# Two-layer encoder on one core: the first output tile beside the last heads, and the norms by halves of the positions

## The reference, cut to what matters

```
mods   = silu(c) @ ada_w + ada_b                 # shifts, scales, gates: rows of channels
layer 0:  h = rmsnorm(x, g) * (1 + scale) + shift
          x = x + gate1 * (forgetting_attention(h) @ w_o)   # 16 heads, causal, bias F_i - F_j
          h = rmsnorm(x, g) * (1 + scale) + shift
          x = x + gate2 * ((silu(conv(h Wg)) * conv(h Wv)) @ w_down)   # 2816 hidden channels
shared:   h = modulated rmsnorm(x);  k, v = h @ kv_w        # 4 heads of 64 channels
layer 1:  q = modulated rmsnorm(x) @ w_q
          x = x + gate1 * (sliding_window_attention(q, k, v, alibi, sinks) @ w_o)
          x = x + gate2 * conv_ffn(modulated rmsnorm(x))
out    =  rmsnorm(x, g)
```

## Time and profile before

| what | us |
|---|---|
| device time, median of three runs | 2446.96 |
| the three runs | 2446.95, 2446.96, 2448.36 |
| device time of the profiled execution | 2450.65 |
| span of the profiled execution in the trace | 2448.8 |
| PE busy | 2309.4 |
| DVE busy | 1535.8 |
| POOL busy | 1173.5 |
| ACT busy | 1147.6 |

### The profile page before, as it was taken

One profiled execution on the slowest core, in us unless ns is written; L12 is line 12 of the kernel. 1 busy time (PEld: TensorE's weight loads), 2 busy tenths in 40 slices (PEclk: granted clock), 3 DMA queues, 4 the chain that ended last, 5 costly groups with the idle time before them and its releaser, 6 DMA issues.

```text
span 2448.8 us, 30449 instructions
## 1 busy us (share of the span) xinstructions
PE 2309.4 (94%) x10984; PEld 1922.2 (78%) x10984; DVE 1535.8 (63%) x2470; ACT 1147.6 (47%) x1934; POOL 1173.5 (48%) x1580
## 2 busy tenths in 40 slices
PE   5999999998989999999999899989899999999996
PEld 3778788886767888888888688878678888888884
DVE  6575656657677677777665686882564444545546
ACT  4475665748145333333333476771443333333334
POOL 5411313120546766666666352214366666666650
PEclk8999999999999999999999999989999999999998
DMA  7111211112831333333331313133111111111111
GB/s 266 53 48 35 69 35 55 42 56 78 309 112 42 117 121 121 121 125 123 124 119 59 127 34 77 53 110 122 35 43 52 52 52 57 56 52 52 52 52 69
DMA packets 66007, 206.91 MB, mean 84 GB/s; under 512 B 7345, under 2 KB 7985, under 8 KB 65730
## 3 DMA queue, kind: packets, MB, share of 16 engines
q1 hardware_dynamic: 29760, 109.06, 14.0%
q10 hardware_dynamic: 36098, 95.91, 12.0%
HBM read 186.66 MB, written 16.32 MB: 83 GB/s over the span
## 4 chain that ended last, share of the span: by engine, by line
PE 80%; DVE 9%; ACT 6%; DMA 3%; issue 2%; SPq 0%; POOL 0%; ACTq 0%; DVEq 0%
PE bank L917 50%; PE bank L632 19%; PE bank L792 1%; PE bank L766 1%; DVE H L1658 1%; PE bank L827 1%; PE bank L802 1%; PE bank L1088 1%; PE bank L828 1%; PE bank L829 1%; ACT PF L1226 1%; DMA ada_raw<-in_ada_t 1%; PE bank L648 1%; DVE tn L1653 1%; DVE ada_raw L1669 1%
## 5 line engine op out<-in xcount | busy, mean ns | idle before, releaser
L917 PE MATMUL bank<-H,w_spl 128*128 128x512 f32 x3744 | 872.3, 392 | 19.3 <-DVE H L1658 14.6
L917 PEld LDWEIGHTS bank<-H,w_spl 128*128 128x128 f32 x3744 | 708.0, 189 | 171.7 <-issue 16.2
L561 POOL TENSOR_TENSOR w_spl<-w_raw,w_spl 128x256 fp32r<-128x256 f32 x688 | 536.7, 808 | 426.7 <-ACT w_spl L1380 425.2
L632 PE MATMUL bank<-H,w_spl 128*128 128x512 f32 x2016 | 509.9, 401 | 19.1 <-DVE H L1658 11.6
L917 PE MATMUL bank<-TB,w_spl 128*128 128x512 f32 x2112 | 492.6, 389 | 0.0
L917 PEld LDWEIGHTS bank<-TB,w_spl 128*128 128x128 f32 x2112 | 396.1, 188 | 83.3 <-issue 0.8
L632 PEld LDWEIGHTS bank<-H,w_spl 128*128 128x128 f32 x2016 | 378.4, 193 | 98.1 <-issue 12.6
L1380 ACT ACTIVATE w_spl<-w_raw 128x512 fp32r<-128x512 f32 x328 | 196.8, 624 | 356.3 <-PE bank L917 300.5
L499 POOL TENSOR_TENSOR pace<-one_s 128x1 f32<-128x1 f32 x50 | 13.1, 262 | 682.9 <-PE bank L792 350.5
L1934 DVE SCALAR_TENSOR_TENSOR X<-bank,mods,X 128x1024 f32<-128x1024 f32 x176 | 225.2, 1280 | 45.5 <-PE bank L917 44.7
L1927 DVE TENSOR_TENSOR bank<-bank,sU 128x512 f32<-128x512 f32 x80 | 55.9, 699 | 302.6 <-PE bank L917 302.6
(11 more groups left out here) (172 smaller groups left out, 3180.1 us busy)
## 6 DMA issues: line engine op xcount, KB each, us to landing
w_raw<-in_w_stream SPq DMA_DIRECT2D x184, 512.0 KB, 3.7
ada_raw_f<-in_ada_t ACTq DMA_DIRECT2D x128, 256.0 KB, 2.9
ada_raw_o<-in_ada_t ACTq DMA_DIRECT2D x8, 2048.0 KB, 7.7
ada_raw<-in_ada_t SPq DMA_DIRECT2D x8, 1024.0 KB, 18.9
negF<-scratch_f ACTq DMA_DIRECT2D x16, 512.0 KB, 3.7
X<-in_x_t SPq DMA_DIRECT2D x4, 1024.0 KB, 10.9
X<-in_x_t ACTq DMA_DIRECT2D x4, 1024.0 KB, 8.3
scratch_x<-X ACTq DMA_DIRECT2D x1, 4096.0 KB, 12.7
```

Source lines behind the costliest of these rows:

```text
L561: last = pool.tensor_tensor(block_at(layer, b, 1, q, q + 256), src[:, q:q + 256], block_at(layer, b, 0, q, q + 256).bitcast(F32), ALU.subt ...
L632: last = pe.matmul(dst, stat(k, a), mov(k, b), start=(k == 0 and a + b == 0), stop=(k == KT - 1 and a == 1))
L917: last = pe.matmul(dst, block_at(layer, b, x, k * P, k * P + P), mov(y), start=(start and x + y == 0), stop=(stop and x == 1), skip_group_ ...
```

## The change

1. **Heads.** All heads take one plan of maxima (MAX_T), the negated maxima always at t = 8, and four of the 32 fill steps move from the second head of a group to the first (FILL_1).
2. **The last group.** From T = 20 POOL makes the high parts PH (POOL_HIGH), in parts of 256 columns, in ACT's place. O is loaded (HEADS_LOADS) and split (HEADS_SPLITS) earlier, straight into H's place. PE puts seven of the eight k-steps of the output projection's tile 0 (six matmuls each) beside the tasks (OUT_A_BESIDE); out_two then makes tile 1 and ends both. POOL's weight tiles from the fourth of w_o on come after its high parts.
3. **Output projections.** Tiles 6 and 7 go by halves of the positions (out_last), and the sum of the first half's squares, its root, its norm and its modulation begin before the second halves are done; the FFN's first pair also goes by halves, with the second half's sum inside it. Tiles 4 to 7 make three rows of mods instead of four; the four others go into FFN pairs 2 and 3 as half rows, and the other half rows move from pairs 3 to 18 to pairs 4 to 19 (ada_steps).
4. **FFN entry.** The taps of hidden tile 0 move ahead of the last two of the four T sums, on ACT and DVE; hidden tile 0's split moves behind the copy that S4 waits for.
5. **FFN end and K/V.** The last down product goes by halves in a ring of four banks (last_down), residuals by halves, POOL adds the squares (add_squares, two operations of 256 columns for each), and the norm and the K/V product go by halves. This norm writes X × rstd into X itself, so that the norm for Q has no multiplication. SP stores X in halves before that, and loads bias_s, both of which were on ACT's queue.
6. **The end.** DVE multiplies X by gain and rstd in one operation into Y, in 16 halves, and SP issues 16 DMAs of 256 KB.

```diff
-MAX_T = [[2, 1, 1, 1, 1, 1, 1, 2, 2, 0, 0, 0], [0, 0, 2, 1, 2, 1, 2, 1, 2, 1, 0, 0]]
-MAX_T.append(MAX_T[0])
+MAX_T = [2, 1, 1, 1, 1, 1, 1, 2, 2, 0, 0, 0]
...
-FILL_1 = [2] * 16
+FILL_1 = [3] * 4 + [2] * 10
...
+POOL_HIGH = 20
+HEADS_LOADS = {13: (0, 1, 2), 14: (3, 4, 5), 34: (6,)}
+HEADS_SPLITS = {16: 0, 18: 1, 20: 2, 22: 3, 24: 4, 26: 5, 41: 6}
+OUT_A_BESIDE = {25: (0,), 28: (1,), 31: (2,), 34: (3,), 37: (4,), 40: (5,), 44: (6,)}
...
+def ada_steps(p):
+    if p in (2, 3):
+        return 4 * (p - 2), 4, p - 2, p == 2
+    if 4 <= p < 20:
+        return 8 + 8 * (p - 4), 8, int(p < 12), p < 12
+    return 136, 0, 0, False
...
+            def store_x(h):
+                for j in range(4):
+                    sp.wait_ge(dn_ev, 80 + 8 * h + 2 * j + 2)
+                    sp.dma_start(dX.rearrange("k p s -> p k s")[:, 2 * j:2 * j + 2, half_of(h)],
+                                 X[:, 2 * j:2 * j + 2, half_of(h)]).then_inc(x_out[h], 16)
             for pos in range(3, W_TILES):
+                if pos in (W_KV + 2, W_KV + 3):
+                    store_x(pos - W_KV - 2)
+                if pos == W_KV + 3:
+                    sp.dma_start(bias_s[:], alibi).then_inc(bias_in, 16)
...
+            for h in range(2):
+                for kt in range(KT):
+                    sp.wait_ge(y_done, 8 * h + kt + 1)
+                    sp.dma_start(out_t[kt, :, half_of(h)], Y[:, kt, half_of(h)]).then_inc(y_out, 16)
+            sp.wait_ge(y_out, 16 * 16)
...
+            for T in range(POOL_HIGH, 4 * NT):
+                n_task = 4 * NT * (NG - 1) + T
+                n = task_span(T % NT)[1]
+                pool.wait_ge(p_exp, n_task + 1)
+                for q in range(0, n, 256):
+                    last = pool.tensor_scalar(PH[n_task % NP][:, q:min(n, q + 256)], PF[n_task % NP][:, q:min(n, q + 256)],
+                                              1.0, 1.0, ALU.mult, ALU.mult)
+                last.then_inc(p_hi, 1)
+            for pos in range(W_OUT_A + 3, W_FFN[0]):
+                tile(pos)
...
+            def add_squares(n, m, h):
+                pool.wait_ge(sq_done, SQ_0[n] + 8 * h + m + 1)
+                first = ss[:, half_of(h)]
+                if m == 1:
+                    first = sq_at(n, 0, h)
+                else:
+                    pool.wait_ge(ss_done, SS_0[n] + 6 * h + m - 1)
+                for q in (0, 256):
+                    last = pool.tensor_tensor(ss[:, h * HALF + q:h * HALF + q + 256], first[:, q:q + 256],
+                                              sq_at(n, m, h)[:, q:q + 256], ALU.add)
+                last.then_inc(ss_done, 1)
...
+            def square_sum(n, h):
+                at_end = n == 4 and h == 1
+                pe.wait_ge(ss_done, SS_0[n] + (6 * h + 6 - at_end if n in (2, 4) else 6 + h))
+                pe.matmul(bank(h), ones[:], ss[:, half_of(h)], start=True, stop=False)
...
+                pe.wait_ge(sq_done, SQ_0[n] + (8 * h + 8 if n in (2, 4) else 8 + 2 * h))
+                pe.matmul(bank(h), ones[:], sq_at(n, 7, h), start=False, stop=True).then_inc(sum_ps, 1)
...
+            def out_first(layer, ks):
+                for k in ks:
...
+                    pe.wait_ge(o_lo, 8 * layer + k + 1)
+                    out_step(layer, 0, k, int(k == 0) * layer)
...
+            def out_last(layer):
+                for h in range(2):
+                    for m in (LAST, LAST + 1):
+                        if h == 0:
+                            pe.wait_ge(w_ready, tile_order([W_OUT_A, W_OUT_B][layer] + m) + 1)
+                            pe.wait_ge(wo_ev, 10 * layer + m - 1)
+                        for k in range(KT):
+                            last = product(bank(4 + 2 * ((m + 1) % 2) + h), w_tile([W_OUT_A, W_OUT_B][layer] + m),
+                                           h_cols(h * HALF, HALF), [k], release=int(k == 0 and (m == LAST) != (h == 1)))
+                            if k == KT - 1:
+                                last.then_inc(wo_ps, 1)
+                            if h == 1 and m == LAST and k == SUM_OUT:
+                                square_sum(1 + 2 * layer, 0)
+            def out_two(layer, ks):
+                out_first(layer, ks)
+                pe.wait_ge(w_ready, tile_order([W_OUT_A, W_OUT_B][layer] + 1) + 1)
+                if layer:
+                    pe.wait_ge(o_addB, 64)
+                else:
+                    pe.wait_ge(p_exp, NT * NH)
...
-                    for k in range(KT):
...
+                    for h in range(2):
+                        for k in range(KT):
+                            if h == 0 and k % 4 == 0:
+                                pe.wait_ge(b_ready, n0 + 2 * (k // 4) + 2)
+                            pe.wait_ge(h_lo, H_0[[1, 4][layer]] + 8 * h + k + 1)
+                            for gv in range(2):
+                                for x, y in ((0, 0), (0, 1), (1, 0)):
+                                    last = pe.matmul(bank(2 * gv + h), block_at(layer, 2 * (k // 4) + gv, x, k % 4 * P,
+                                                                                k % 4 * P + P),
+                                                     H[:, k, y, half_of(h)], start=(k == 0 and x + y == 0),
+                                                     stop=(k == KT - 1 and x == 1), skip_group_check=True)
...
+                            if h == 0 and k == SUM_NEXT[1 + 2 * layer]:
+                                square_sum(1 + 2 * layer, 1)
+                    used[0] = 2
...
+                def last_down():
+                    it = FT // 2 - 1
+                    for hh in range(2):
+                        for m in range(8):
...
+                            if hh == 1 and m == SUM_DOWN:
+                                square_sum(2 + 2 * layer, 0)
...
+                for kv, k in [(0, 0), (0, 1), (1, 0), (1, 1)] + [(i % 2, i // 2) for i in range(4, 2 * KT)]:
+                    if kv == 0:
...
+                if layer == 0:
+                    mods_of_tile(LAST + 1)
+                    dve.wait_ge(ada_step, ADA_2)
+                coefficients(hn)
+                dve.wait_ge(x_in[3], 32 + 16 * layer)
+                residual(LAST, 0)
+                add_squares(n, LAST - 1)
+                add_squares(n, LAST, 0)
+                residual(LAST + 1, 0)
+                half_scaled(hn, 0, 0)
+                half_scaled(hn, 1, 0)
+                residual(LAST, 1)
+                half_low(hn, 0, 0)
...
+                residual(LAST + 1, 1)
+                for k in range(3, KT):
+                    half_low(hn, k, 0)
+                    if k + 2 < KT:
+                        half_scaled(hn, k + 2, 0)
+                second_half(hn)
...
+                    if kk == 2:
+                        taps(0, 0, pair(0))
+                        taps(0, 1, pair(2))
                     t_sums(kk)
...
+                dve.wait_ge(rs_done, 1 + 2 * 3 + h + 1)
+                for k in range(KT):
+                    V_.scalar_tensor_tensor(Y[:, k, half_of(h)], X[:, k, half_of(h)], gain[:, G_FIN + k:G_FIN + k + 1],
+                                            rstd[:, half_of(h)], ALU.mult, ALU.mult).then_inc(y_done, 1)
```

639 lines of the change are left out of this document (387 added, 252 removed).

## The result

The changed kernel takes 2424.88 us (median of four runs, 2420.87 to 2428.93), the kernel before beside it 2447.66; the ratio is 0.9905, 95% interval 0.9886 to 0.9924. It is faster by some 23 us where 62.5 were forecast, and lies above the range. The runs of one kernel spread wider than the three of the kernel before had shown: 8 us here. The profiled execution took 2420.87 us with a span of 2418.8, against 2450.65 and 2448.8 before: 30 us between the two traces.

A forecast was written before the change was run, and what follows sets the result against it. PE's matmuls bound the kernel (2309.4 of 2448.8 us), so only its gaps could be won: heads −9, tile 0 +1, FFN entries −10 and −11, K/V and Q −22, end −11.5, in all −62.5, giving 2384 us (2371 to 2397).

The forecast's parts named there:

- the maxima plan: Attention heads: one plan of maxima for all heads wins 2 us a head, 8 us over four groups.
- POOL's high parts: Last two heads: 46 parts on POOL at 0.418 us each, hidden, freeing ACT; 1 us won for this tail.
- The loss of 7 us: Last two heads: if POOL and DVE shut each other out, 48 us against 40.5, and the time 2392.
- Tile 0: First output projection: k-steps beside the heads win nothing, the third tile's wait grows to about 12.6 us; +1 us.
- FFN entries: Behind both output projections: S4 62.0 us after the last matmul instead of 73.2; −10 and −11 us.
- K/V and Q: Between the first FFN's end and Q: idle time, waits and slow clock go; −22 us, range −10 to −26.
- The end: From the last down product's start to the kernel's end: 39.3 us instead of 50.8; −11.5 us.
- Edges eat half: Whole kernel: half operations' starts, semaphores and in-order DVE and ACT leave −35 us, 2412; chance 0.20.
- Slower: Last 28 attention tasks: POOL's high parts set the pace, at 2.6 us a part about 2453 us; chance 0.03.

The follow-up runs named there:

- the control: The changed kernel run again without an edit, beside its edited versions: 2420.20 us, ratio 0.9878 to the kernel before.

## Why the prediction was wrong

**Heads: the maxima plan, a step that failed.** It was priced at 2 us a head from the difference of heads 2 and 3 with the fill taken off. The excess was the place: in the second and third group second heads are as long with either plan, and the 2.7 us that they lost is the moved fill, which the first heads took on.

**Heads: O's loads and splits, a step that was missing.** They were named as an edit and not priced. In the second head of the last group they cost 7.3 us (30.3 against 23.0), of which the later heads get back 5.

**Heads: POOL's high parts, right in price, wrong in use.** 36 parts of 256 columns took 0.515 us each and 10 of 128 columns 0.495, near the lower end, and hidden. But ACT was not what the inserted k-steps needed. The heads are as long without POOL's parts. The loss of 7 us worked out by the rule of the Trainium skill (SBUF — State Buffer, "SBUF: two separate sides") did not show.

**Tile 0: the wait right, the price not.** The wait at the third tile was forecast at 12.6 us and is 12.85, the third tile 25.2 us after the last value and is 25.3. The last two heads took 41.9 and 40.4 us, within the 43.4 that they were said to fit in. But without tile 0 they take 35.7: its price was put at 1 us and is 4.7, since only half of it fitted beside the tasks.

**FFN entries: the chain behind the T sums, mis-sized.** Forecast was S4 62 us behind the projection; it is 71.9. The second half's multiplication starts 12.3 us after the last matmul, not 10.5. The two operations of its root were put at 2.2 us, the price of full width, and take 1.3; but its sum ends at 7.7 us instead of 6.3, and ACT begins the root 3.3 us after that. The eight halves take 13.4 us to the first T sum, not 10.8, for ACT begins a half only every 1.43 to 1.46 us; and from the first T sum to S4 it is 46.2 us, where 40.7 were forecast. This last 5.5 is the larger part. The forecast took the 2.4 us of wait at S4 off for the later split of hidden tile 0, and gave the taps that move ahead no price. The runs show that these put a wait of 7.5 before S2 and cost some 3 us, and that weight splits and, in FFN 0, a half row's load stand behind that. What holds FFN 0's S3 once all these are moved was not tried further.

**K/V and Q: the sum near, the shares not.** Together they won 18.9 us of 22, but by two misses of opposite sign, which is luck. K/V won 5.9 where 13.5 were forecast: PE still waits 4.3 us in steps, all for DVE's low parts of H, and from 1400 to 1412 us the clock is 0.86. POOL's sums came at the price forecast (0.84). What was left out is what they do to DVE: from 1399 to 1409 us, with POOL busy 9.6 of 10 us, DVE is busy 9.8, and its half multiplications take 1.22 us instead of 0.69 (see the last section). That this is what holds K/V is read from the trace; no run took the sums off POOL. Q won 13.0 where 8.5 were forecast. The windows at Q, two of the kernel before and two of the changed one, show why:

```profile
1455.00:1475.00 20.00, 15.69 (x53) 10.95 (x52) 13.49 (x15) 12.42 (x15) 11.71 (x11) 0.83 0.46 111
1475.00:1500.00 25.00, 21.79 (x114) 18.58 (x112) 13.48 (x55) 11.62 (x45) 7.04 (x15) 0.86 0.27 74
...
1455.00:1475.00 20.00, 20.00 (x97) 16.47 (x96) 10.90 (x33) 10.01 (x28) 9.84 (x18) 1.00 0.65 152
1475.00:1500.00 25.00, 24.82 (x162) 22.22 (x161) 20.90 (x81) 18.50 (x67) 4.93 (x9) 1.00 0.08 22
```

Before, PE lost 15.69 × 0.17 + 21.79 × 0.14 = 5.7 us there to the clock, beside 7.5 of waits: 13.2. The forecast gave the clock 1. After, both windows run at 1.00.

**The end: right.** 38.0 us against 39.3 forecast; 16 operations on Y take 10.68 us, and POOL's sums, at 0.74 us an operation, hold PE for 0.9 once.

**The rivals.** "Edges eat half" at 2412 was nearest, and its mechanism, ACT and DVE in order, is what the FFN entries show. Its shares were not met: the heads lost 4 us where it had a gain of 4, and K/V with Q won 18.9 where it had 12. The argument against it was misread from the earlier trace rows: ACT is busy 8.26 of 13.5 and 8.25 of 15.0 us there, more than half. Only "Slower" had the heads getting longer, by POOL's high parts, which did not hold them.

## What to carry to other kernels

Work that is moved into an engine's gaps is only won if what comes next was waiting for that engine; here the third tile waited for a load, and tile 0 beside the heads cost 5 us. An engine that works in order carries a removed wait on to its next instruction, as the 7.5 us at S2 came back as 10.5 at S4, so the chain must be followed to the end of the stage before it is priced. Loads and splits that are moved to an earlier time are an edit with a price of their own, to be read from what those queues do at the new place.

## What the runs showed of the hardware that was not expected

DVE's half operations with two operands in SBUF are slower while POOL works. Groups by form of the changed kernel, first from 708 to 722 us (POOL busy 11.8 of 14 us), then from 722 to 737 (POOL busy 1.4 of 15):

```profile
L1915 DVE TENSOR_TENSOR tnFh<-X,rstdF 128x512 f32<-128x512 f32 x6 | 6.5, 1089 | 0.0
L1920 DVE TENSOR_TENSOR H<-TBf,H 128x512 fp32r<-128x512 f32 x6 | 6.2, 1029 | 0.1
L2138 DVE SCALAR_TENSOR_TENSOR X<-bank,mods,X 128x512 f32<-128x512 f32 x2 | 1.5, 746 | 0.1
...
L1915 DVE TENSOR_TENSOR tnFh<-X,rstdF 128x512 f32<-128x512 f32 x9 | 6.5, 731 | 0.5 <-ACT rstdF L1348 0.5
L1920 DVE TENSOR_TENSOR H<-TBf,H 128x512 fp32r<-128x512 f32 x9 | 6.2, 691 | 2.8 <-ACT H L1377 2.4
```

1.03 to 1.09 us against 0.69 to 0.73, while the residual, with one operand in a bank, stays at 0.75. The same holds in all 17 traces of the changed kernel and its edits: these two operations take 1.09 to 1.12 us (median) where POOL works for more than 80% of their time, and 0.69 where it is idle. A run that takes POOL's work away shows it too, in the last two heads: DVE's low parts PL of 128x512 take 0.77 us in the control and 0.69 where ACT makes the high parts. POOL pays as well: its low parts of weights (L633) take 1.07 us from 708 to 722, against a mean of 0.82 over the whole kernel.

The Trainium skill (SBUF — State Buffer, "SBUF: two separate sides") has the two engines share a port pair as an exclusive lock against such operations; the trace agrees that they hold each other up. At the FFN entry and in K/V this falls on DVE in the chain from the root to H; no run moved POOL's work away there, so what it costs the whole kernel is not shown.
